# The attention-heads loop of a two-layer block: other places for the side jobs of a head pair

## The reference

```
q = rms(rms(cq) * q_norm @ w_uq) * q_gain              # per head, 96 = 64 + 32 rotary
k = rms([k_nope, k_rope]) * k_gain                     # k_nope, v from rms(ckv) * kv_norm @ w_ukv
k, v cover 256 context + 512 latent tokens; rotary on q and on the latent k_rope
out = softmax(q @ k.T * 96**-0.5) @ v                  # per block of 128 queries, all 768 keys
y = out @ w_out
```

## Time and profile before

| what | value |
|---|---|
| median of three runs | 3747.44 us |
| the profiled execution | 3746.08 us, span 3744.3 us |
| TensorE busy | 3609.9 us (96%) |
| VectorE, ScalarE, GpSimd busy | 1743.5, 1506.9, 1277.3 us |
| mean granted TensorE clock | 0.99 of 2.4 GHz |

### The profile page before, as it was taken

How to read it: one execution, slowest core, us unless ns; L and a number is a source line. 1 busy time by engine, 2 the same in 40 slices (tenths; PEclk the granted TensorE clock), 3 DMA queues, 4 the chain that set the end, 5 groups by cost and what they waited for, 6 DMA issues and landing times.

```text
span 3744.3 us, 53306 instructions
## 1 busy us (share of the span) xinstructions
PE 3609.9 (96%) x19978; PEld 2906.3 (78%) x19978; DVE 1743.5 (47%) x2548; ACT 1506.9 (40%) x2525; POOL 1277.3 (34%) x540
## 2 busy tenths in 40 slices
PE   7999999999999999999999999999989999999998
PEld 5875788888877767888777788688867777878886
DVE  4766652333357766343555543411165555252114
ACT  4343432222356663233655543322245555233222
POOL 2530332232321114444423334344432323434443
PEclk9999999999999999999999999999999999999999
DMA  5368211111210002222212112222222111222222
GB/s 208 117 220 301 80 68 68 62 62 62 84 57 23 29 21 98 101 96 95 85 68 68 68 68 101 74 96 95 99 74 69 63 69 68 91 84 90 95 97 88
DMA packets 84708, 333.82 MB, mean 89 GB/s; under 512 B 9520, under 2 KB 9648, under 8 KB 78000
## 3 DMA queue, kind: packets, MB, share of 16 engines
q1 hardware_dynamic: 83808, 329.22, 25.1%
q10 hardware_dynamic: 720, 2.10, 0.2%
HBM read 329.18 MB, written 2.10 MB: 88 GB/s over the span
## 4 chain that ended last, share of the span: by engine, by line
PE 77%; issue 12%; DVE 6%; POOL 3%; ACT 2%; POOLq 0%; DVEq 0%; ACTq 0%
PE pB L276 16%; PE pB L277 16%; PE pB L278 16%; PE pB L2317 14%; POOL w_lo L2882 3%; PE pO L276 1%; PE pO L278 1%; PE pO L277 1%; PE pT L278 1%; PE pT L277 1%; PE pT L276 1%; PE pT L2375 1%; DVE arena L903 1%; PE pO L2402 1%; DVE small L1956 1%
## 5 line engine op out<-in xcount | busy, mean ns | idle before, releaser
L2882 POOL TENSOR_TENSOR w_lo<-w_raw,w_hi 128x1024 fp32r<-128x1024 f32 x520 | 1261.0, 2427 | 2344.9 <-ACT w_hi L322 2344.4
L276 PE MATMUL pB<-h_hi,w_hi 128*128 128x512 f32 x2084 | 821.9, 394 | 37.9 <-DVE h_lo L2810 15.3
L277 PE MATMUL pB<-h_lo,w_hi 128*128 128x512 f32 x2084 | 816.1, 392 | 0.0
L278 PE MATMUL pB<-h_hi,w_lo 128*128 128x512 f32 x2084 | 815.0, 391 | 0.0
L322 ACT ACTIVATE w_hi<-w_raw 128x1024 fp32r<-128x1024 f32 x520 | 547.9, 1054 | 480.6 <-PE pB L278 315.0
L276 PEld LDWEIGHTS pB<-h_hi,w_hi 128*128 128x128 f32 x2084 | 394.8, 189 | 131.2 <-issue 39.1
L278 PEld LDWEIGHTS pB<-h_hi,w_lo 128*128 128x128 f32 x2084 | 394.6, 189 | 83.1
L277 PEld LDWEIGHTS pB<-h_lo,w_hi 128*128 128x128 f32 x2084 | 395.1, 190 | 79.9 <-issue 0.7
L276 PE MATMUL pB<-b_hi,w_hi 128*128 128x512 f32 (+1 forms) x1084 | 399.7, 369 | 4.6 <-POOL w_lo L2882 2.6
L277 PE MATMUL pB<-b_lo,w_hi 128*128 128x512 f32 (+1 forms) x1084 | 394.9, 364 | 0.0
L278 PE MATMUL pB<-b_hi,w_lo 128*128 128x512 f32 (+1 forms) x1084 | 394.6, 364 | 0.0
(11 more groups left out here) (548 smaller groups left out, 5188.5 us busy)
## 6 DMA issues: line engine op xcount, KB each, us to landing
w_raw<-stream SPq DMA_DIRECT2D x520, 512.0 KB, 3.2
under<-ada SPq DMA_DIRECT2D x42, 1024.0 KB, 4.9
arena<-ada SPq DMA_DIRECT2D x6, 1024.0 KB, 17.4
x<-xT SPq DMA_DIRECT2D x1, 2048.0 KB, 8.8
out<-x SPq DMA_DIRECT2D x8, 256.0 KB, 2.1
xc<-cT SPq DMA_DIRECT2D x1, 1024.0 KB, 26.7
arena<-bmask ACTq DMA_DIRECT2D x1, 1024.0 KB, 4.7
arena<-brope ACTq DMA_DIRECT2D x2, 256.0 KB, 5.3
```

The lines of the kernel that those rows point to most:

```text
L276: pe.matmul(dst, lh, rh, start=(begin and k == 0), stop=False)
L277: pe.matmul(dst, lh, rl, start=False, stop=False)
L278: last = pe.matmul(dst, ll, rh, start=False, stop=(end and k == len(pairs) - 1))
L2882: pool.tensor_tensor(w_lo[:, s, :], w_raw[:, s, :], w_hi[:, s, :].bitcast(F32), ALU.subtract).then_inc(lo_ready, 1)
```

## The change

The same jobs are made, in another order. In the heads loop AV and R of pair `p-1` move behind the first Q of pair `p` and swap places; the Q that stood at `s == 5` of the pair before moves to that pair start; the other Q goes from `s == 3` to 2, SK and SC from 2 to 3, V jobs one step on. VectorE and ScalarE get their parts of these jobs at other steps. Before the loop the context chunks run in one piece, ScalarE's work is put in another order, and the rotary part of the keys is done earlier on VectorE. The core of the diff (hunk headings in words; left out are the waits on `kr_step`, whose numbers follow the order, and that `dve_rope_keys` goes ahead of `dve_mla_const` and of the norm of ckv_lat):

```diff
@@ turns_beside: where the side jobs of the next pair stand @@
-            ahead = [("Q", 2 * q + 2)] if q + 1 < PAIRS_A else []
-            return [[("K", q)], [("C", q)] + values[0:1], values[1:2] + [("SK", q), ("SC", q)], [("Q", 2 * q + 1)], [("SQ", q)],
-                    ahead, values[2:3], []]
+            return [[("K", q)], [("C", q)] + values[0:1], [("Q", 2 * q + 1)], [("SK", q), ("SC", q)], values[1:2] + [("SQ", q)],
+                    values[2:3], [], []]
+        def turn_ahead(p):
+            return [("Q", 2 * p + 2)] if 0 < p < PAIRS_A - 1 else []
...
         for _p in range(PAIRS_A):
+            TURNS_A += turn_ahead(_p)
+            if _p:
+                TURNS_A += [("AV", _p - 1), ("R", _p - 1)]
             for _row in turns_beside(_p):
                 TURNS_A += _row
-            TURNS_A += [("R", _p), ("AV", _p)]
+        TURNS_A += [("AV", PAIRS_A - 1), ("R", PAIRS_A - 1)]
@@ pe_mla_heads: the same order, written out @@
             for p in range(PAIRS_A):
+                for turn in turn_ahead(p):
+                    pe_turn(pe, turn)
+                if p:
+                    pe_turn(pe, ("AV", p - 1))
+                    pe_turn(pe, ("R", p - 1))
...
-                    if p % 2 == 0 and s == 6:
+                    if p % 2 == 0 and s == 5:
...
-                pe_turn(pe, ("R", p))
-                pe_turn(pe, ("AV", p))
+            pe_turn(pe, ("AV", PAIRS_A - 1))
+            pe_turn(pe, ("R", PAIRS_A - 1))
@@ act_mla_heads @@
+                for turn in turn_ahead(p):
+                    act_turn(act, turn)
+                if p:
+                    act_turn(act, ("R", p - 1))
...
-                    if s == 4 and p + 1 < PAIRS_A:
+                    if s == 5 and p + 1 < PAIRS_A:
                         act_key_high(act, n)
+                    for turn in beside[:-1]:
+                        act_turn(act, turn)
                     if u + 2 < UNITS:
                         act_unit_exp(act, u + 2)
-                    for turn in beside:
+                    for turn in beside[-1:]:
                         act_turn(act, turn)
...
-                        if s == 1:
+                        if s == 2:
                             act_query_high(act, n)
...
+                        if s == 7:
+                            act_key_high(act, n + 1)
@@ dve_mla_heads, inside the pair loop @@
-                if p:
-                    dve_pair_scale(dve, p - 1)
+                if 0 < p < PAIRS_A - 1:
+                    dve_query_turn(dve, 2 * p + 2)
...
                     dve_unit_copy(dve, u)
+                    if s == 0 and 0 < p < PAIRS_A - 1:
+                        dve_pair_scale(dve, p - 1)
...
+                        if s == 0:
+                            dve_query_rope(dve, n)
                         if s == 2:
+                            dve_query_turn(dve, n + 1)
+                        if s == 3:
+                            dve_query_rope(dve, n + 1)
                             dve_query_low(dve, n)
-                        if s == 3:
+                        if s == 4:
                             dve_key_scale(dve, n)
-                        if s == 4:
+                        if s == 5:
                             dve_key_low(dve, n)
-                            dve_query_turn(dve, n + 1)
-                        if s == 5:
-                            dve_query_rope(dve, n + 1)
-                        if s == 6 and p + 2 < PAIRS_A:
-                            dve_query_turn(dve, n + 2)
-                        if s == 7:
+                        if s == 6:
                             dve_key_scale(dve, n + 1)
+                        if s == 7:
                             dve_query_low(dve, n + 1)
                             dve_key_low(dve, n + 1)
...
@@ dve_mla_heads, before the loop: the norm of ckv_ctx goes behind both query turns @@
             dve_query_turn(dve, 0)
-            dve_norm(dve, "ckv_ctx", tile_of(ckv, C), C, TC, lambda kt: col("kv_norm", kt), None, (*H, 0))
             dve_query_rope(dve, 0)
             dve_query_turn(dve, 1)
             dve_query_rope(dve, 1)
-            dve_rope_keys(dve)
+            dve_norm(dve, "ckv_ctx", tile_of(ckv, C), C, TC, lambda kt: col("kv_norm", kt), None, (*H, 0))
             dve_rope_context(dve)
@@ pe_mla_in @@
-            ctx_chunk(0)
-            ctx_chunk(1)
+            for j in range(3):
+                ctx_chunk(j)
             pe_norm(pe, "ckv_lat", T)
-            ctx_chunk(2)
@@ act_mla_in @@
             evacuate(6)
-            act_hi_part(act, g0 + 9)
             act_rope_squares(act, 1, ev(g0 + 6))
             act_root(act, "cq", T)
+            highs("cq", T, None, (*B, KD * C))
+            evacuate(7)
             for kt in range(2):
                 act_square(act, "ckv_lat", kt, lambda k: ckv[:, k, C:TC], T)
-            for kt in range(4):
-                act_high(act, "cq", kt, T, T, None, (*B, KD * C))
-                if kt == 1:
-                    act_hi_part(act, g0 + 10)
+            evacuate(8)
+            evacuate(9)
             act_root(act, "ckv_lat", T)
...
@@ act_mla_heads, FIRST_TURNS, behind ("Q", 1) @@
                         act_high(act, "ckv_ctx", kt, C, TC, None, (*H, 0))
+                    act_rope_squares(act, 0, ev(G_MLA[1] + 2))
```

More of the change, by code:

```diff
@@ L1720, in pe_turn @@
             elif what == "SK":
-                pe.wait_ge(kr_step, 1)
+                pe.wait_ge(kr_step, 4)
                 pe.wait_ge(k_total, 2 * n + 1)
@@ L1938, in act_mla_heads @@
                         act_pair_high(act, p - 1)
+                    g = G_HEADS + 3 * (p // 2)
                     if p + 1 < PAIRS_A:
-                        if s == 1:
+                        if s == 2:
                             act_query_high(act, n)
@@ L1947, in act_mla_heads @@
                             act_hi_part(act, g + (4 if s == 4 else 5))
-                act_turn(act, ("R", p))
-                if p + 1 < PAIRS_A:
-                    act_key_high(act, n + 1)
+            act_turn(act, ("R", PAIRS_A - 1))
             act_pair_high(act, PAIRS_A - 1)
@@ L2036, in dve_rope_keys @@
             dve.tensor_scalar(kr[NOPE:P, C:TC], kr[NOPE:P, C:TC], gain, None, ALU.mult).then_inc(kr_step, 1)
-            dve.wait_ge(kr_step, 2)
+            dve.wait_ge(kr_step, 1)
             dve.tensor_tensor(mt1[r, :], kr[r2, C:TC], sinm[r2, :], ALU.mult)
             dve.tensor_tensor(kr[r, C:TC], kr[r, C:TC], cosm[r, :], ALU.mult).then_inc(kr_step, 1)
-            dve.wait_ge(kr_step, 3)
+            dve.wait_ge(kr_step, 2)
             dve.tensor_tensor(kr[r, C:TC], kr[r, C:TC], mt1[r, :], ALU.add).then_inc(kr_step, 1)
@@ L2079, in dve_mla_heads @@
                     u = 8 * p + s
+                    n = 2 * p + 2
                     if u + 2 < UNITS:
@@ L2172, in act_mla_in @@
             evacuate(6)
-            act_hi_part(act, g0 + 9)
             act_rope_squares(act, 1, ev(g0 + 6))
             act_root(act, "cq", T)
+            highs("cq", T, None, (*B, KD * C))
+            evacuate(7)
             for kt in range(2):
                 act_square(act, "ckv_lat", kt, lambda k: ckv[:, k, C:TC], T)
-            for kt in range(4):
-                act_high(act, "cq", kt, T, T, None, (*B, KD * C))
-                if kt == 1:
-                    act_hi_part(act, g0 + 10)
+            evacuate(8)
+            evacuate(9)
             act_root(act, "ckv_lat", T)
-            for j in (7, 8):
-                act.wait_ge(chunk_done, done(g0 + j))
-                act.activation(places[j], bank[(g0 + j) % SLOTS][:, 0:C], ACT.Copy).then_inc(evac[(g0 + j) % SLOTS], 1)
             for kt in range(2):
-                act_square(act, "ckv_ctx", kt, lambda k: ckv[:, k, 0:C], C, ev(g0 + 7 + kt))
+                act_square(act, "ckv_ctx", kt, tile_of(ckv, C), C)
             highs("ckv_lat", TC, None, (*H, C))
-            act_hi_part(act, g0 + 11)
-            act.wait_ge(chunk_done, done(g0 + 9))
-            act.activation(places[9], bank[(g0 + 9) % SLOTS][r, 0:C], ACT.Copy).then_inc(evac[(g0 + 9) % SLOTS], 1)
-            act_rope_squares(act, 0, ev(g0 + 9))
             act_hi_part(act, G_HEADS + 2)
@@ L3052, in _ @@
             dve_norm(dve, "cq", tile_of(cq), T, T, lambda kt: col("q_norm", kt), None, (*B, KD * C))
+            dve.wait_ge(rope_in, 32)
+            dve_rope_keys(dve)
             dve_mla_const(dve)
-            dve.wait_ge(rope_in, 32)
             dve_norm(dve, "ckv_lat", lambda kt: ckv[:, kt, C:TC], T, TC, lambda kt: col("kv_norm", kt), None, (*H, C))
```

10 lines of the change are left out of this document (3 added, 7 removed).

## The result

| | before | after |
|---|---|---|
| median of four runs each | 3748.22 us | 3786.33 us |
| lowest to highest | 3746.08 to 3750.64 | 3781.79 to 3787.68 |
| ratio, 95% interval | | 1.0099 [1.0085, 1.0114] |
| span of the profiled execution | 3744.3 | 3785.0 |
| sums of the norms (L461) to the scores of unit 2 | 53.48 | 60.22 |

The kernel got slower by 38.1 us. 3773.5 was forecast: the direction and the large waits were right, the size was 13 us short. The measured time lies 0.3 us above the 3786 that closed the range for 8 in 10, and 6 above the forecast's own range. The two stretches in the table make 6.74 + 33.48 = 40.2 of the 40.7 us between the profiled executions. The remainder is scatter of work that the change does not touch: the sums start at 1067.08 before and 1070.11 after, and the stretch behind the loop takes 2343.4 and 2340.8.

The account below looks back on a forecast made before the run. TensorE's standing still was taken to bound the kernel. Loop 20, work before the heads 4.4 and clock 1.6 made +26, so 3773.5 us; own range 3766 to 3780, range for 8 in 10 3757 to 3786.

Parts of the forecast that it names:

- What bounds the kernel: Whole kernel: 77% of the span hangs on TensorE, so its standing still counts; VectorE and ScalarE are not full.
- (a): Pair start: the first Q hides the copy AV waits for, taking away 1.60 us (0.28 in even pairs).
- (b): K's bank, pairs 1 to 6: VectorE's multiplication reading AV comes late, so K is 2.0 us late, 12 us.
- (c): Second Q's bank: ScalarE and VectorE free it late, so SC starts 0.65 us late, only in pairs without V jobs.
- (d): Next pair's first scores: they wait for VectorE's low part of the key, 3.1 us in odd pairs, about 1.2 in even.
- (e): Key's low part on VectorE: GpSimd's low part of a weight chunk slows it, 0.6 us in odd pairs, 0.7 in even.
- (f): Steps 6 and 7: late copies cost 0.45 us at step 7's transposes and 0.45 at AV; 3.3 behind pair 6.
- Before the heads: Before the loop: TensorE waits 3.7 us at chunk 9 and the first Q is 2.8 later; +4.4 in all, 2 to 7.
- The clock: Behind new waits of 3.1 to 3.7 us: the clock falls, costing 1.6 us over the loop, bounds 0 and 9.
- The sum over the loop: Heads loop: odd pairs +3.55 three times, even pairs +2.0 twice, pairs 0, 6 and 7 +5.4; in all +20 us.
- The rival with its clock falling after each long wait: Loop and before: about 1.7 us in seven pairs, the full 5.2 before the loop; +37, 3784, chance 0.15.
- The other rivals: Key path not late, 3761 (0.15); pair start hides more than it costs, 3740 (0.04); gains and waits cancel, about 3751 (0.05).

Follow-up runs that it names:

- e8: The kernel before, with VectorE's last copy of pT put ahead of the maximum in steps 2 and 7: 3746.08 us, 0.9995.
- e9: The kernel before, with VectorE's last copy of pT put ahead of the maximum in step 7 alone: 3740.63 us, 0.9987.
- e3: The changed kernel, with the multiplication that reads AV put directly behind the query turn on VectorE, ahead of step 0's maximum: 3769.35 us, 1.0058.
- e7: The changed kernel, with SK, SC, second Q, their key work and the V jobs back at their old steps: 3764.54 us, 1.0049.
- e1: The changed kernel with the old order before the loop, so only the heads loop is changed: 3779.1 us, 1.0087.
- e6: The changed kernel, with ScalarE's high part of chunk 9's weights back ahead of the norm of cq: 3784.1 us, 1.0097.
- e5: The changed kernel, with overwritten filler matmuls on TensorE ahead of a pair's first scores (15, or 6 in even pairs) and K (7): 3775.73 us, 1.0078.
- e11: The changed kernel, with ScalarE's high part of weight chunks moved from step 4 (and 6) to step 7 (6 and 7): 3777.02 us, 1.0081.
- e4: The changed kernel, with SK, SC, second Q and their key work back at old steps, V jobs left as changed: 3779.93 us, 1.0090.

## Why the prediction was right, and where its size was not

**What bounds the kernel** held. The loss is TensorE standing still for VectorE, plus its clock; no engine became full.

**(a)** Right: no AV that has a Q ahead of it waits by 0.4 or more, and e8 and e9 show the same 1.60 to be mostly a matter of one copy (0.49 is left).

**(b)** Right, 2.0 us late in six pairs. The rows show 1.70 of idle time, counted from the modelled end of the row before; from start to start it is 2.0. e3 took all six away by moving one instruction.

**(c)** Too high: the second Q's bank costs 0.20 to 0.22, not 0.65. There is none in pair 0. That is 2 us over the four pairs.

**(d)** Right in place and releaser. 3.1 + 0.6 of (e) was forecast for odd pairs and 4.0 measured from start to start (3.77 idle); 1.2 + 0.7 for even ones, and 1.8 (1.53 idle). VectorE's list could be added up in advance from the rows of before. e7 shows what it is worth, 22.4 us of loop with its clock (18.9 against e1's).

**(e)** Right in kind. It cost 0.75 in odd pairs (0.6 assumed) and 0.6 in even ones (0.7 assumed). By the Trainium skill, GPSIMD Engine Reference, section Specifications, VectorE instructions contend with GpSimd if they have two SBUF inputs or run in a 2-port mode. The rows agree: the maximum at 1193.00 and the copy at 1194.12, both from PSUM, lie under the same GpSimd job and take their usual 0.96 and 0.55.

**(f)** Right in the large wait, AV behind pair 6: 2.91 idle (3.3 forecast), and in the last AV, 0.85 (0.9). The two of 0.45 in steps 6 and 7 were too high: 0.15 and 0.17 at the transposes of two pairs, nothing at AV.

**Before the heads**: 3.7 forecast at chunk 9 and 3.83 measured. The sum +4.4 was low, +6.74 came out: chunk 9 ran at half the clock behind its wait and took 5.3 us instead of 3.4, so the first Q started 5.6 later and not 2.8; and SR waits 3.80 instead of the 3.02 of the earlier trace rows. The half clock behind SR was there before too. e6 confirms chunk 9; the rest of this account is read from the rows alone.

**The clock**: this is the step that was mis-sized. It was taken as 1.6 us with a bound of 9. The sum over the loop without it was +20, so 300.4; e5, with the clock held up to AV behind pair 6, measured 302.93, and this AV took 8.0 against 5.2 elsewhere; without these 2.8 it is 300.1. What is above that in after, 313.84 - 300.1 = 13.7, is the clock's by this estimate (10.3 and 10.8 in e1 and e6). It is on the low side, since e5 itself has two jobs at half the clock at its loop's start. Added up from rows of after (the scores, transposes, K and AV at 0.63 a matmul against the same jobs at 0.40) it is 15.9: 2.1 in pair 0, 2.8 in pair 1, 0 in pair 2, 2.6, 1.3, 2.8, 1.5 and 2.8 in pairs 3 to 7. All are above the bound of 9. The error was threefold. I counted four waits of over 3 us, but K lost the clock too in three of six pairs, behind waits of 1.7 to 2.0, and the scores of pair 4 behind one of 1.53. I left out the wait at AV behind pair 6, though (f) had put it at 3.3 us; AV took 2.8 more behind it. And I let most of the slow work hide behind a late VectorE, while it stood on the path.

The rival with its clock falling after each long wait gave 3784 and is next to the measured 3786.3, but its mechanism (about 1.7 in seven pairs, 12 in all) is only partly what was seen: pair 2 kept 1.00, five pairs lost 2.1 us or more, and the stretch before the loop grew by 6.7 instead of 5.2. That it comes so near is partly luck. The other rivals fell: K and the key path were both late.

**What stays open.** Which of the waits of 1.5 to 2.0 us lose the clock, and how soon it falls behind a longer one. And e6's 2.2 us can't be told from nothing.

## What to carry to other kernels

Where engines run fixed lists, work out ahead of a reordering when each engine gets to the instruction that frees a bank or completes an operand, by adding the rows in its list; this gave the large waits (chunk 9, K, the first scores, AV) to within 0.4 us here, and the small ones up to 0.45 too high. Then price each new idle time of the matmul engine twice, once for itself and once for what runs behind it at half the clock, unless that clock is shown to hold. And a stall of 1.6 us at a pair's end was cheaper to mend by swapping two instructions of the engine that was late (e9) than by moving five jobs of the one that waited.

## What the runs showed of the hardware that was not expected

**Every longer wait cost the clock, and shorter ones did at times.** Four loops (after, e1, e3, e6) have sixteen waits of 3.76 to 3.79 us at the first scores of a pair; each was followed by work at 1.2 GHz within two jobs. So were e11's four of 3.0, e4's three of 2.4 at SQ, and the six of 2.9 at AV behind pair 6 (AV 6.5 to 8.2 us instead of 5.2). What varied was the moment. TensorE of e1 in pair 5, behind 3.77 us of idle time:

```profile
1351.04 0.47 PE L1762 MATMUL pS<-mla_k,mla_q 96*128 96x512 f32 x1 [3.77 <-issue]
1351.35 0.39 PE L1763 MATMUL pS<-mla_k,mla_q 96*128 96x512 f32 x1
...
1352.88 0.78 PE L1762 MATMUL pB<-mla_k,mla_q 96*128 96x512 f32 x1
```

It starts at 2.4 GHz and is at 1.2 GHz two jobs later; in pairs 0 and 1 of e1 it was at 1.2 GHz from the start. With the shorter waits it went either way. K took 2.51, 2.25 and 2.72 us in pairs 1, 5 and 6 of after, behind waits of 1.71, 1.70 and 2.01, and 1.49 in the others, behind 1.70. In e7, whose loop has no wait above 2.02, only the K behind 2.02 was slow (2.60). The 1.60 of before was never followed by half clock; the 1.53 to 1.55 at the loop's start, which both kernels have, was so in e3, e5 and e7, and not in before and after. The Trainium skill, TensorE: Matmul & The Clock Gate, section What's actually happening, says that the moment at which the clock rises at a kernel's start varies from run to run. These rows show the like for its fall, between equal pairs of one run.

**Its price here.** 1.2 to 2.9 us for one fall, 10 to 16 us over the loop by the sums above, and 6 to 15 spare matmuls in a gap bought 7.5 to 11 of them back (e5).

**Work that is the same takes a different time.** The stretch behind the loop, with the same code in all kernels, took from 2340.8 to 2347.0 us in fourteen profiled executions. A difference under 6 us between two single traces has to be looked for in the stage that was edited, not in the spans; and where the clock falls in that stage, as in the loop of after, e1 and e6, it alone moved by 3.5.
